# Six weight low parts formed by GpSimd in place of VectorE, in the last attention stage of a one-core kernel

## The reference, cut to what matters

```
def dsa_attention(q, k, v, qi, ki, wi, rel_bias):
    ...                                   # per token t, keys s
    rel = relu(einsum('thd,sd->ths', qi_t, ki))
    score = einsum('ths,th->ts', rel, wi_t) * idx_scale
    score = where(pos[None, :] <= t[:, None], score, -inf)
    _, sel = top_k(score, top_k)          # top_k = 64 of 256
    ...
    logits = einsum('thd,tkhd->thk', q_t, k_sel) * attn_scale + bias
    p = softmax(logits)                   # 16 heads
    return einsum('thk,tkhd->thd', p, v_sel)

    # in the layer
    proj = h @ c_w_in                     # 1024 x 3656, split into q, k, v, qi, ki, wi
    y = dsa_attention(...) @ c_w_out      # 1024 x 1024
```

## Time and profile before

| | |
|---|---|
| median of three runs | 2610.11 us |
| lowest, highest | 2609.17, 2612.05 us |
| profiled execution | 2608.07 us |
| its span (first to last instruction) | 2606.3 us |
| mean granted TensorE clock | 0.980 |
| TensorE busy | 2421.2 us (93%) |
| VectorE busy | 1226.3 us (47%) |
| ScalarE busy | 947.7 us (36%) |
| GpSimd busy | 82.7 us (3%) |

### The profile page before, as it was taken

How to read it: one execution, slowest core, us unless ns; L and a number is a source line. 1 busy time by engine, 2 the same in 40 slices (tenths; PEclk the granted TensorE clock), 3 DMA queues, 4 the chain that set the end, 5 groups by cost and what they waited for, 6 DMA issues and landing times.

```text
span 2606.3 us, 32111 instructions
## 1 busy us (share of the span) xinstructions
PE 2421.2 (93%) x13359; PEld 1673.7 (64%) x13359; DVE 1226.3 (47%) x2012; ACT 947.7 (36%) x1498; POOL 82.7 (3%) x88
## 2 busy tenths in 40 slices
PE   9998787888998888888999999999999999999998
PEld 7742222227842333326988888888888888887887
DVE  5621000007722000006777665775577577587764
ACT  5420000007520000004555445654365465445653
POOL 0001000001001000000000000000200000022000
PEclk9999999999999999999999999999999999999999
DMA  8599999997599999999534445555455555554551
GB/s 282 212 383 427 424 427 429 427 413 260 193 408 425 427 425 426 427 423 265 189 109 149 167 146 186 178 194 189 143 180 192 194 180 192 177 183 146 178 184 67
DMA packets 227537, 692.35 MB, mean 266 GB/s; under 512 B 30281, under 2 KB 130673, under 8 KB 201280
## 3 DMA queue, kind: packets, MB, share of 16 engines
q1 hardware_dynamic: 225152, 684.87, 69.6%
q0 software_dynamic: 2240, 5.42, 0.7%
HBM read 686.84 MB, written 5.28 MB: 266 GB/s over the span
## 4 chain that ended last, share of the span: by engine, by line
PE 65%; DMA 19%; DVE 7%; ACT 4%; issue 1%; SPq 1%; PEld 0%; POOL 0%; DVEq 0%; POOLq 0%; ACTq 0%; PEldq 0%
PE accumulators L584 26%; PE accumulators L2002 12%; PE accumulators L3774 12%; DMA weight_ring<-in_moe_w_gate 8%; DMA weight_ring<-in_moe_w_up 7%; PE accumulators L3775 6%; DMA weight_ring<-in_moe_w_down 2%; DVE weight_lows L293 2%; ACT weight_highs L284 1%; PE accumulators L1865 1%; PE accumulators L3095 1%; SPq L458 1%; PE accumulators L329 1%; PE accumulators L2982 1%; DMA bias_rows<-work 1%
## 5 line engine op out<-in xcount | busy, mean ns | idle before, releaser
L293 DVE TENSOR_TENSOR weight_lows<-weight_ring,weight_highs 128x1024 fp32r<-128x1024 f32 (+1 forms) x503 | 600.9, 1221 | 314.3 <-ACT weight_highs L284 309.7
L284 ACT CAST weight_highs<-weight_ring 128x1024 fp32r<-128x1024 f32 (+1 forms) x503 | 511.9, 1043 | 244.2 <-PE accumulators L584 224.4
L2002 PE MATMUL accumulators<-weight_ring,arena 128*32 128x512 f32 x1952 | 448.8, 622 | 84.6 <-DMA weight_ring<-in_moe_w_gate 44.9
L3774 PE MATMUL accumulators<-xT_halves,weight_highs 128*128 128x512 f32 x1408 | 492.0, 394 | 1.0 <-DVE xT_halves L892 0.8
L3775 PE MATMUL accumulators<-xT_halves,weight_lows 128*128 128x256 f32 x1408 | 393.7, 280 | 0.0
L2002 PEld LDWEIGHTS accumulators<-weight_ring,arena 128*32 128x32 f32 x1952 | 127.1, 114 | 386.2 <-issue 385.8
L584 PE MATMUL accumulators<-weight_highs,arena_halves 128*128 128x512 f32 x1040 | 328.2, 392 | 2.2 <-DVE arena L2842 1.2
L584 PE MATMUL accumulators<-xT_halves,weight_highs 128*128 128x256 f32 (+3 forms) x1584 | 302.5, 293 | 5.8 <-DVE xT_halves L1194 2.5
L3774 PEld LDWEIGHTS accumulators<-xT_halves,weight_highs 128*128 128x128 f32 x1408 | 264.0, 187 | 62.0 <-issue 1.7
L3775 PEld LDWEIGHTS accumulators<-xT_halves,weight_lows 128*128 128x128 f32 x1408 | 265.6, 189 | 0.0
L584 PEld LDWEIGHTS accumulators<-xT_halves,weight_highs 128*128 128x128 f32 (+3 forms) x1584 | 251.7, 195 | 14.5 <-issue 8.5
(11 more groups left out here) (500 smaller groups left out, 2203.5 us busy)
## 6 DMA issues: line engine op xcount, KB each, us to landing
weight_ring<-in_moe_w_down SPq DMA_DIRECT2D x56, 2048.0 KB, 17.9
weight_ring<-in_moe_w_up SPq DMA_DIRECT2D x54, 2048.0 KB, 19.3
weight_ring<-in_moe_w_gate SPq DMA_DIRECT2D x51, 2048.0 KB, 18.1
weight_ring<-in_ffn_w_gate SPq DMA_DIRECT2D x44, 1024.0 KB, 5.1
weight_ring<-in_ffn_w_up SPq DMA_DIRECT2D x44, 1024.0 KB, 5.2
weight_ring<-in_ffn_w_down SPq DMA_DIRECT2D x44, 1024.0 KB, 4.8
weight_ring<-in_l_w_in SPq DMA_DIRECT2D x38, 1024.0 KB, 5.0
weight_ring<-in_moe_w_gate SPq DMA_DIRECT2D x18, 1024.0 KB, 4.8
```

The source lines that it names most:

```text
L284: act.copy(p.high(), p.raw()).then_inc(self.high_ready, 1)
L293: dve.tensor_tensor(p.low(), p.raw(), p.high().bitcast(F32), ALU.subtract).then_inc(self.low_ready, 1)
L2002: last = pe.matmul(acc[e * CAP:(e + 1) * CAP, half * BANK:(half + 1) * BANK], tokens, stream.part(first + e, c)[:, half * BANK:(half + 1) ...
L3774: pe.matmul(acc, high, m.xT_r[:, c, :, :].rearrange("p k t -> p (k t)"), start=(c == 0), stop=False, skip_group_check=True)
```

## The change: what it does, and the diff

Six low parts, pieces 6, 8, 10, 12, 14 and 16, are subtracted by GpSimd instead of VectorE, with the same operands. GpSimd counts them on a new semaphore, `pool_low_ready`; TensorE waits on it for these six, and for the others on `low_ready` less the number of GpSimd pieces that come before. VectorE's `lows` passes over them. On GpSimd the four subtractions of pieces 6, 8, 10 and 12 stand after the bias DMAs of the first two pairs and before `factored` of unit 2; those of 14 and 16 stand between `factored` of unit 2 and of unit 3. No other operation changes.

```diff
+        self.pool_low_ready = ctx.enter_context(nc.semaphore("pool_low_ready"))
+        self.pool_pieces = []
...
         while self.lows_made < min(end, len(self.pieces)):
             p = self.pieces[self.lows_made]
-            dve.wait_ge(self.high_ready, p.n + 1)
-            dve.tensor_tensor(p.low(), p.raw(), p.high().bitcast(F32), ALU.subtract).then_inc(self.low_ready, 1)
             self.lows_made += 1
+            if p.n not in self.pool_pieces:
+                dve.wait_ge(self.high_ready, p.n + 1)
+                dve.tensor_tensor(p.low(), p.raw(), p.high().bitcast(F32), ALU.subtract).then_inc(self.low_ready, 1)
+
+    def pool_low(self, pool, n):
+
+        p = self.pieces[n]
+        pool.wait_ge(self.high_ready, n + 1)
+        pool.tensor_tensor(p.low(), p.raw(), p.high().bitcast(F32), ALU.subtract).then_inc(self.pool_low_ready, 1)
...
     def wait(self, eng):
-        eng.wait_ge(self.stream.m.low_ready, self.n + 1)
+        m = self.stream.m
+        by_pool = sum(n < self.n for n in m.pool_pieces)
+        if self.n in m.pool_pieces:
+            eng.wait_ge(m.pool_low_ready, by_pool + 1)
+        else:
+            eng.wait_ge(m.low_ready, self.n + 1 - by_pool)
...
+POOL_LOWS = ((2, 2), (2, 6), (3, 2), (3, 6), (4, 2), (4, 6))
...
             for i in range(len(units)):
                 heads.load(pool, s, i)
                 if i == 1:
+                    lows = [in_stream.at(u, c).n for u, c in POOL_LOWS]
+                    for piece in lows[0:4]:
+                        m.pool_low(pool, piece)
                     factored(K[0])
+                    for piece in lows[4:6]:
+                        m.pool_low(pool, piece)
                     factored(Q[0])
...
-            ColumnStream(m, a["c_w_in_3"][0], C_UNITS)
+            stream = ColumnStream(m, a["c_w_in_3"][0], C_UNITS)
+            m.pool_pieces += [stream.at(u, c).n for u, c in POOL_LOWS]
```

## The result

| | before | changed |
|---|---|---|
| median | 2610.19 us (7 runs) | 2618.25 us (7 runs) |
| lowest, highest | 2608.84, 2612.05 | 2615.31, 2623.57 |
| ratio | | 1.0034, interval 1.0025 to 1.0043 |
| profiled execution, span | 2608.07, 2606.3 | 2623.57, 2621.8 |

The change makes the kernel 8.1 us slower. The forecast was +2.9 us with a range up to 2617.5, so it had the sign right and the size wrong, and the time lies outside its range.

What follows compares the result with a forecast made beforehand. The prediction took VectorE to bound the stage from 2305.96 to 2343; -1.14 us for piece 16 and +4.1 for GpSimd holding the adds gave +2.9, so 2610.11 + 2.9 = 2613.0 us, range 2607.0 to 2617.5.

Steps and rivals of the forecast that it cites:

- What bounds the stage: TensorE bounds the stage up to 2305.4, VectorE from 2305.96 to 2343; VectorE's changes until 2337.10 move the end one for one.
- only piece 16 gives anything back: Of six subtractions leaving VectorE, only piece 16's, at 2314.83, lies on the path: 1.14 us saved.
- The cost of one subtraction: Each GpSimd subtraction of 128x1024 was taken as 2.36 us, between 1.22 and 3.25 us.
- Before 2305.96: Early GpSimd subtractions delay the adds of heads 0 and 1, but VectorE is level by 2302.0: 0, at most 0.5 us.
- the prediction's signs of being wrong: L4394 starting by 2311, TensorE waiting for L293 or GpSimd between 2289 and 2305, or unhindered GpSimd operations over 3 us.
- In that gap the port is free.: At the adds of heads 6 and 7, each waits for the one before, leaving GpSimd a gap for piece 14, 2.36 us.
- its early count: Adds of heads 0 and 1, first at 2294.25, pushed back about 0.5 us behind piece 10, up to 2.4 behind 12.
- At the adds: From 2305.96, `factored` (0.74 us) and subtractions of 14 and 16 (2 x 2.36) hold VectorE; `choose` begins 4.1 us later.
- TensorE's first wait: Wait before the turn of the first pair, for the weights of L3050: 2.13 us, forecast to grow to about 5.0.
- The clock: Slow stretch at 0.52 from 2344.0 to 2347.4: taken as unchanged, 0; a second +1.7 us, none on the path -1.7.
- that the port goes to VectorE first each time: Rival at the adds: queued VectorE work wins, 14 and 16 run under `choose`; gain 1.8 us, 2608.3 us, chance 0.20.
- A slower GpSimd: Rival: GpSimd takes 3.25 us per subtraction and piece 6 is 0.1 late; +4.7 us, 2614.9, chance 0.09.

## Why the prediction was wrong, point by point

- *What bounds the stage*, and that only piece 16 gives anything back: right. From L4416 to `limit` it is 21.2 us after, from L4394 to `limit` 22.3 before, 1.1 us less.
- *The cost of one subtraction*, 2.36 us: right; the row of three takes 7.00, the kernel's six lie between 2.34 and 2.63 us.
- *Before 2305.96: "I count nothing", with at most 0.5 us.* This step failed: it cost +7.3 us, 4.9 of waiting and 2.4 of slow clock. The error of the profiled execution, 4.8 us, is this less 0.9 at the adds and 1.6 of the clock, below. TensorE did wait in the stretch that the prediction's signs of being wrong named, but for L2862, not for L293 or GpSimd. I had written that "GpSimd and a VectorE instruction with two SBUF inputs, or L3050, exclude each other", and L3050 is a TENSOR_SCALAR. I did not go through what else of that kind stands in VectorE's queue between 2286 and 2296. The row was there to read: L4379 at 2285.63, 0.9 us before the forecast start of the first subtraction. By itself it costs 0.29 us; the price came from its place, ahead of L2848 and of TensorE. The Trainium skill lists `tensor_scalar` among the operations that can take the shared pair ("SBUF — State Buffer", section "Who interferes with whom"); the trace agrees, 7.82 us for 128x2.
- *"In that gap the port is free."* The prediction said this of the adds, and there it was right in part: the first add got in ahead of a ready subtraction, and GpSimd took the gaps behind the first and the third. But the same picture lies under its early count ("about 0.5 us behind 10, then up to 2.4 behind 12", one operation at a time), and there it fails: three in a row hold the small instruction for 7.8 us, not 3.2. With waits between them, TensorE waits 0.3 us instead of 4.8.
- *At the adds*: the mechanism was right, the size a little high. The sum had 1.89 us of work and 0.74 + 2 x 2.36 = 5.46 us of being held for the four adds, 7.35 together; measured 6.46. Three adds were held, and they are longer than their own 0.35 or 0.48 us by 0.5, 2.0 and 2.0: a held add ends 0.15 to 0.3 us behind the GpSimd record, less than its own length. So the masked score came 3.2 us later by this step, not 4.1, and with piece 16 the late part is +2.1, not +2.9. TensorE's first wait did not grow to about 5.0: it is 2.96, with a new one of 1.04 ahead of it.
- *The clock*: I took 0 and gave +1.7 or -1.7 as the alternatives. Both happened: a new slow stretch on the path behind the new wait (2.4), and the old one moved under VectorE (-1.6). That the old one moved so was luck: I had named the possibility, but nothing that decides it, and in three of the experiments the stretch is absent behind the same two waits.
- *The rivals*: that the port goes to VectorE first each time is refuted by the row of three and by the gaps that GpSimd took between the adds. A slower GpSimd is refuted by its rows. No rival was what happened: the hold of a VectorE instruction that I had not listed.

## What to carry to other kernels

Before work goes to GpSimd, list every VectorE instruction in the window that has two SBUF inputs or is a tensor_scalar within SBUF, however small, and ask who waits behind it. For a tensor_scalar, price the whole row of GpSimd work that is ready, not one instruction; for the others one instruction is what these runs show, and the row is the upper bound. Put such work beside VectorE instructions that do not share the port (MAX8, MATCH_REPLACE8, a TENSOR_TENSOR with one input in PSUM), held back by a semaphore if need be, and let GpSimd wait for its own result where VectorE must get in. Here the same kind of operation in the same stage cost 8.1 us in one place and gained 4.0 us in another.

## What the runs showed of the hardware that I had not expected

- GpSimd keeps a waiting TENSOR_SCALAR out through all subtractions that stand ready: 3.23, 5.53, 7.82 us for a row of 1, 2, 3. A wait of GpSimd on its own result (0.3 us over three subtractions) lets it in behind the first. A SCALAR_TENSOR_TENSOR of 128x128 got in between `factored` and a ready subtraction without such a wait (0.86 us).
- A ready subtraction holds the port from 0.5 to 0.8 us or more before its record starts, while GpSimd is still issuing DMAs; the DMAs alone do not (0.24 us).
- TensorE's wait of 4.84 us was followed by 5.7 us at 0.52 of the full clock, which cost half as much again as the wait: 2.4 us. A wait of 1.39 us also had a slow stretch behind it (0.57 over 3.4 us), one of 0.26 us had none. The two waits at the first turn and the first answer, 2.1 to 2.2 us and 1.8, had a slow stretch behind them in the kernel before and none in three others.
